# The last expert's rows kept on chip, and the residual summed by adding DMAs, in a one-core hybrid decoder step

## The reference

```python
def hier_moe(h, w_rg, b_rg, w_re, b_re, w_gate, w_up, w_down):
    ...
    g_sel = jnp.argmax(glog, axis=-1)                    # 1 of 4 groups
    ...
    top_v, top_i = lax.top_k(elog_sel, TOP_K_IN_GROUP)   # 2 of its 8 experts
    w_top = jax.nn.softmax(top_v, axis=-1) * p_g
    ...
    for e in range(N_EXPERTS):                           # 32, D_EXPERT = 512
        a = jax.nn.silu(hf @ w_gate[e]) * (hf @ w_up[e])
        y = y + gates[:, e:e + 1] * (a @ w_down[e]).astype(jnp.float32)
    ...

x = x + jnp.concatenate([yc, yp], axis=-1) @ w_out
x = x + hier_moe(rmsnorm(x, g_ffn), w_rg, b_rg, w_re, b_re, w_gate, w_up, w_down)
y = rmsnorm(x, g_final)
```

## Time and profile before

| what | value |
|---|---|
| median of 3 runs | 1410.45 us (1408.94 to 1411.17) |
| the profiled execution's own time | 1409.55 us |
| its span, first to last instruction | 1407.8 us |
| granted TensorE clock, mean | 0.978 of full speed |
| busy: TensorE / DVE / ACT / GpSimd | 1250.1 / 344.2 / 121.3 / 116.5 us |
| DMA | 464.61 MB, mean 330 GB/s |
| down product of the last expert ends | 1356.8 us |

### The profile page before, as it was taken

How to read it: one execution, slowest core, us unless ns; L and a number is a source line. 1 busy time by engine, 2 the same in 40 slices (tenths; PEclk the granted TensorE clock), 3 DMA queues, 4 the chain that set the end, 5 groups by cost and what they waited for, 6 DMA issues and landing times.

```text
span 1407.8 us, 16671 instructions
## 1 busy us (share of the span) xinstructions
PE 1250.1 (89%) x6515; PEld 711.9 (51%) x6515; DVE 344.2 (24%) x677; ACT 121.3 (9%) x242; POOL 116.5 (8%) x166
## 2 busy tenths in 40 slices
PE   8999989999999999989988898998898998898850
PEld 7777767777875444444333443433344343344210
DVE  4299953011251110110101011010111101011017
ACT  1100013000100000000000000000000000000003
POOL 2211143000000000000000000000000000000004
PEclk9999999999999999999999999999999999999985
DMA  8533423566349999999999999999999999999964
GB/s 233 163 120 119 153 86 107 198 247 243 133 190 373 421 423 426 423 422 421 424 423 423 424 421 423 422 423 424 422 423 422 424 421 424 420 423 419 379 193 124
DMA packets 100790, 464.61 MB, mean 330 GB/s; under 512 B 10095, under 2 KB 52207, under 8 KB 62115
## 3 DMA queue, kind: packets, MB, share of 16 engines
q1 hardware_dynamic: 95088, 455.89, 81.1%
q0 software_dynamic: 5392, 7.86, 1.8%
q10 hardware_dynamic: 283, 0.48, 0.1%
HBM read 456.67 MB, written 20.80 MB: 339 GB/s over the span
## 4 chain that ended last, share of the span: by engine, by line
DMA 50%; PE 35%; issue 7%; DVE 6%; SPq 1%; ACT 0%; ACTq 0%; DVEq 0%; POOLq 0%
DMA arena<-in_w_up_dram 48%; PE bank L546 13%; PE bank L699 13%; PE bank L718 3%; DVE arena L931 3%; PE bank L678 2%; PE bank L494 1%; DMA arena<-expert_rows 1%; SPq L381 1%; DMA pv<-in_pool_scale_dram 1%; PE bank L613 1%; DVE arena L1179 1%; DVE tn L891 0%; PE bank L583 0%; PE bank L630 0%
## 5 line engine op out<-in xcount | busy, mean ns | idle before, releaser
L699 PE MATMUL bank<-arena,stage 128*64 128x512 f32 x1920 | 429.4, 595 | 74.3 <-DMA arena<-in_w_up_dram 74.3
L699 PEld LDWEIGHTS bank<-arena,stage 128*64 128x64 f32 x1920 | 139.4, 137 | 356.7 <-issue 293.4
L546 PE MATMUL bank<-arena,stage 128*128 128x288 f32 x1280 | 315.0, 407 | 0.8 <-DVE arena L914 0.8
L546 PEld LDWEIGHTS bank<-arena,stage 128*128 128x128 f32 x1280 | 241.9, 190 | 66.3 <-issue 0.9
L678 PEld LDWEIGHTS bank<-x1w,x1r 96*128 96x128 f32 x1536 | 174.0, 192 | 26.0 <-issue 26.0
L678 PE MATMUL bank<-x1w,x1r 96*128 96x128 f32 x1536 | 180.2, 277 | 0.0
L1150 DVE TENSOR_TENSOR a_sb<-sl_sb,bank 128x256 f32<-128x256 f32 x32 | 19.4, 606 | 504.8 <-ACT sl_sb L843 504.8
L718 PE MATMUL bank<-arena,aT 128*64 128x512 f32 x512 | 113.4, 595 | 8.5 <-ACT aT L845 8.5
L1292 POOL DMA_INDIRECT expert_rows<-ysb,cur_d x32 | 31.3, 978 | 882.1 <-DVE ysb L1159 880.7
L931 DVE SCALAR_TENSOR_TENSOR arena<-arena,wdw 128x256 f32<-128x256 f32 x240 | 103.0, 501 | 0.0
L1159 DVE COPY ysb<-bank 128x512 f32<-128x512 f32 x32 | 22.1, 691 | 261.3 <-PE bank L718 261.3
(11 more groups left out here) (212 smaller groups left out, 494.2 us busy)
## 6 DMA issues: line engine op xcount, KB each, us to landing
arena<-in_w_gate_dram SPq DMA_DIRECT2D x112, 1024.0 KB, 17.0
arena<-in_w_up_dram SPq DMA_DIRECT2D x112, 1024.0 KB, 25.5
arena<-in_w_down_dram SPq DMA_DIRECT2D x30, 2048.0 KB, 21.5
xT<-in_w_down_dram SPq DMA_DIRECT2D x15, 2048.0 KB, 24.1
stage<-in_w_down_dram SPq DMA_DIRECT2D x15, 2048.0 KB, 25.5
stage<-in_w_in_dram SPq DMA_DIRECT2D x11, 2048.0 KB, 8.3
stage<-in_w_out_dram SPq DMA_DIRECT2D x8, 2048.0 KB, 8.1
stage<-in_w_gate_dram SPq DMA_DIRECT2D x16, 512.0 KB
```

The costliest lines, as they stand in the source:

```text
L546: last = pe.matmul(ps[bank][:, 0:NTOK], wsl[a][:, k, cc * P:(cc + 1) * P], rhs[:, k, :], start=(n == 0), stop=(n == KT - 1))
L699: last = pe.matmul(ps[4 + s][BLK * h:BLK * (h + 1), :], xgT[:, k, BLK * s:BLK * (s + 1)], w[:, :, 256 * h:256 * (h + 1)], start=(k == 0), ...
```

## The change

Four things are changed together.

1. **The residual goes to DRAM.** During the projection ACT copies each step's token rows from PSUM to a staging buffer and writes them to a new DRAM tensor `xres_dram` (12 copies of 96x512, four writes).
2. **Gate weights are applied at eviction.** The gate weights are worked out before the table; a second table `wslot` with the weight of each slot is multiplied by TensorE next to the first. ACT and DVE evict banks 2 and 3 with a multiplication by the slot's weight.
3. **The last expert's rows stay on chip**, in `ylast`. Its places in `yexp_dram` are filled with zeros by one more scatter, after the first pair. A one-hot matrix `lastT` (slots x tokens) is made in the last pair. After the experts TensorE multiplies it with `ylast`, 12 products of 96x512.
4. **DMAs add.** SP loads the residual rows into `yg` as each chunk comes free. GpSimd then issues six DMAs of 96 rows x 8 KB that add the rows of `yexp_dram` to them: the first expert row for the three tiles, then the second. DVE adds TensorE's products to the sum and applies norm and gain; GpSimd and ACT do no scaling of rows any more. The last tile goes out in two halves.

```diff
+PARTB = ((0, 1, 6, 7), (4, 5, 0, 1), (6, 7, 4, 5))
...
+        ylast = words(lns, 0, D // 2)
...
+            sp.wait_ge(xres_out, 16 * 4)
+            for t in range(TT):
+                sp.wait_ge(gu_used, 4 * (NE - 1) + t + 1)
+                sp.dma_start(yg[:, t, 0, :], xres_dram[t * TR:(t + 1) * TR, :]).then_inc(res_in[t], 16)
             sp.wait_ge(gu_used, 4 * NE)
             sp.dma_start(gfin, g_final[None, :].to_broadcast([TR, D])).then_inc(gfin_in, 16)
-
-            for s in range(2):
-                sp.wait_ge(y_out[s], 16 * PAIRS)
-            by_token = yexp_dram.rearrange("(t c) d -> t (c d)", c=4)
-            for t in range(TT):
-                for c in range(2):
-                    sp.dma_start(yg[:, t, c, :], by_token[t * TR:(t + 1) * TR, c * D:(c + 1) * D]).then_inc(yg_in[2 * t + c], 16)
-            for t in range(TT):
-                sp.wait_ge(scaled, t + 1)
-                if t == TT - 1:
-                    sp.wait_ge(out_ready, 1)
-                if t < TT - 1:
-                    sp.dma_start(y_prompt[0, t * TR:(t + 1) * TR, :], yg[:, t, 0, :]).then_inc(fin_out, 16)
-                else:
-                    sp.dma_start(y_prompt[0, t * TR:SEQ, :], yg[0:LASTP, t, 0, :]).then_inc(fin_out, 16)
-                    sp.dma_start(y_sample.rearrange("b t d -> (b t) d"), yg[LASTP:TR, t, 0, :]).then_inc(fin_out, 16)
-            sp.wait_ge(fin_out, 16 * (TT + 1))
+            for t in range(TT - 1):
+                sp.wait_ge(out_ready, t + 1)
+                sp.dma_start(y_prompt[0, t * TR:(t + 1) * TR, :], yg[:, t, 0, :]).then_inc(fin_out, 16)
+            t = TT - 1
+            ys_rows = y_sample.rearrange("b t d -> (b t) d")
+            for c in range(2):
+                sp.wait_ge(out_ready, TT + c)
+                d0, d1 = c * (D // 2), (c + 1) * (D // 2)
+                sp.dma_start(y_prompt[0, t * TR:SEQ, d0:d1], yg[0:LASTP, t, 0, d0:d1]).then_inc(fin_out, 16)
+                sp.dma_start(ys_rows[:, d0:d1], yg[LASTP:TR, t, 0, d0:d1]).then_inc(fin_out, 16)
+            sp.wait_ge(fin_out, 16 * (TT + 3))
...
+            pe.wait_ge(row_copy, 4 * TT)
...
-                        pe.wait_ge(dst_ready, 1)
+                        pe.wait_ge(dst_ready, 2)
...
+                    if last and s == 0:
+                        pe.wait_ge(last_ready, 1)
+                        for t in range(TT):
+                            ins = pe.transpose(ps[7][:, t * TR:(t + 1) * TR], last_hot[0][:, t, :], ident[0:TR, 0:TR])
+                        ins.then_inc(last_mm, 1)
...
-                            last = pe.matmul(ps[7][:, 0:NBLK], ohw[:, c, :], ohb[:, c, :], start=(c == 0), stop=(c == 2 * TT - 1))
-                        last.then_inc(tab_mm, 1)
+                            pe.matmul(ps[7][:, 0:NBLK], ohw[:, c, :], ohb[:, c, :], start=(c == 0), stop=(c == 2 * TT - 1))
+                        for c in range(2 * TT):
+                            mm = pe.matmul(ps[7][:, BLK:BLK + NBLK], ohw[:, c, :], ohg[:, c, :], start=(c == 0), stop=(c == 2 * TT - 1))
+                        mm.then_inc(tab_mm, 1)
...
+            pe.wait_ge(lastT_ready, 1)
+            pe.wait_ge(y0_ready, NE)
+            pe.wait_ge(y1_ready, NE)
+            for t in range(TT):
+                for m in range(2):
+                    if t:
+                        pe.wait_ge(part_added, 4 * t + 2 * m - 2 if t == 1 else 4 * t + 2 * m - 4)
+                    for h in range(2):
+                        pe.matmul(ps[PARTB[t][2 * m + h]][0:TR, :], lastT[BLK * h:BLK * (h + 1), t * TR:(t + 1) * TR],
+                                  ylast[BLK * h:BLK * (h + 1), 512 * m:512 * (m + 1)], start=True, stop=True).then_inc(part_mm, 1)
 
...
+            def row_squares(o):
+                for t in range(TT):
+                    if o or t:
+                        act.wait_ge(act_chain, TT * o + t)
+                    act.activation(ysbf[0:TR, 3 * 512:4 * 512], ps[2 + t][0:TR, :], ACT.Square,
+                                   accum_out=ssp3[:, t, o:o + 1]).then_inc(act_chain, 1)
+
+            def row_copies(o):
+                if o:
+                    act.wait_ge(xres_out, 16 * o)
+                for t in range(TT):
+                    if o == 3:
+                        act.wait_ge(row_evac, TT * o + t + 2)
+                    act.copy(ysbf[0:TR, 512 * t:512 * (t + 1)], ps[2 + t][0:TR, :]).then_inc(row_copy, 1)
+
+            def rows_out(o):
+                act.wait_ge(row_copy, TT * (o + 1))
+                act.dma_start(xres_dram.rearrange("(t r) d -> r t d", r=TR)[:, :, 512 * o:512 * (o + 1)],
+                              ysbf[0:TR, 0:512 * TT].rearrange("r (t d) -> r t d", t=TT)).then_inc(xres_out, 16)
+
+            for o in range(4):
                 act.wait_ge(row_mm, 4 * o + 4)
-                for t in range(TT):
-                    act.activation(ysb[0:TR, t % 2, (t // 2) * 512:(t // 2 + 1) * 512], ps[2 + t][0:TR, :], ACT.Square,
-                                   accum_out=dyn(ssp, 4 * t + o, 1, TR)).then_inc(act_chain, 1)
+                if o < 3:
+                    row_copies(o)
+                row_squares(o)
+                if o < 3:
+                    rows_out(o)
             act.wait_ge(act_in, 2)
             act.activation(sq[:, :], va[:, :], ACT.Sqrt).then_inc(sqrt_done, 1)
+            row_copies(3)
+            rows_out(3)
             act.wait_ge(act_in, 3)
             act.activation(r4b[:, :, :], r4[:, :, :], ACT.Exp).then_inc(exp_done, 1)
             act.wait_ge(act_in, 4)
             act.activation(ex[:, :, :], dl[:, :, :], ACT.Exp).then_inc(exp_done, 1)
 
 
-            def pair(i):
+            def pair(i, first=False, last=False):
                 for s in range(2):
                     n = 2 * i + s
-                    act.wait_ge(ysb_free[s], i + 1)
+                    if first and s == 0:
+                        act.wait_ge(xres_out, 16 * 4)
+                    if not (last and s == 1):
+                        act.wait_ge(ysb_free[s], i + 1)
                     act.wait_ge(gu_used, 4 * n + 4)
                     act.activation(sl_sb[:, :], ps[4 + s][:, 0:256], ACT.Silu).then_inc(sl_ready, 1)
                     act.wait_ge(at_mm, n + 1)
                     act.copy(aT[:, :], ps[6][:, 0:256]).then_inc(aT_ready, 1)
+                    if first and s == 0:
+                        act.wait_ge(dst_ready, 2)
+                    if last and s == 1:
+                        act.wait_ge(zero_out, 16)
                     act.wait_ge(wd_used, 4 * n + 4)
-                    act.copy(ysb[:, s, 0:512], ps[2][:, :]).then_inc(y0_ready, 1)
-
-            with act.Fori(0, PAIRS) as i:
+                    to = ylast[:, 0:512] if last and s == 1 else ysb[:, s, 0:512]
+                    act.activation(to, ps[2][:, :], ACT.Copy, scale=dyn(wslot, n, 1)).then_inc(y0_ready, 1)
...
+            act.activation(ssp[:, 0:1], ones[0:TR, 0:1], ACT.Sqrt)
+            for t in range(TT):
+                for c, to in ((0, ss), (1, ssb)):
+                    act.wait_ge(part_added, 4 * t + 4 if c else 4 * t + 3)
+                    act.activation(yg[:, t, 1, c * (D // 2):(c + 1) * (D // 2)], yg[:, t, 0, c * (D // 2):(c + 1) * (D // 2)],
+                                   ACT.Square, accum_out=to[:, t:t + 1]).then_inc(act_chain, 1)
...
+                dve.wait_ge(exp_done, 2)
+                link(dve.tensor_reduce(g2[:, :, :], r4b[:, :, :], AXX, ALU.add))
+                link(dve.reciprocal(pg[:, :, :], g2[:, :, :]))
+                link(dve.tensor_scalar(den[:, :, :], ex[:, :, :], 1.0, None, ALU.add))
+                link(dve.reciprocal(den[:, :, :], den[:, :, :]))
+                w0, w1 = wt[:, 0, :][:, :, None], wt[:, 1, :][:, :, None]
+                link(dve.tensor_tensor(w0, den[:, :, :], pg[:, :, :], ALU.mult))
+                ch.step(dve.tensor_tensor(w1, w0, ex[:, :, :], ALU.mult))
+
...
+                link(dve.tensor_tensor(ohg, ohb, wt[:, :, :].rearrange("p c t -> p (c t)")[:, :, None].to_broadcast([TR, C6, NBLK]), ALU.mult))
...
+                dve.tensor_copy(wslot[:, :], ps[7][:, BLK:BLK + NBLK]).then_inc(dst_ready, 1)
                 dve.tensor_scalar(dst_i[:, :], ps[7][:, 0:NBLK], half[:, :], float(PAD), ALU.add, ALU.add).then_inc(dst_ready, 1)
...
+            def add_part(t):
+                dve.wait_ge(rows_in[t], 32)
+                for m in range(2):
+                    for h in range(2):
+                        n = 4 * t + 2 * m + h
+                        seg = yg[:, t, 0, 1024 * h + 512 * m:1024 * h + 512 * (m + 1)]
+                        dve.wait_ge(part_mm, n + 1)
+                        dve.tensor_tensor(seg, seg, ps[PARTB[t][2 * m + h]][0:TR, :], ALU.add).then_inc(part_added, 1)
+
+            def norm(t):
+                dve.wait_ge(act_chain, 4 * TT + 2 * t + 2)
+                link(dve.tensor_tensor(va[:, t:t + 1], ss[:, t:t + 1], ssb[:, t:t + 1], ALU.add))
```

(60 more changed lines are left out.)

127 lines of the change are left out of this document (52 added, 75 removed).

## The result

| | before | after |
|---|---|---|
| median | 1408.91 us (20 runs) | 1411.03 us (20 runs, 1409.59 to 1414.43) |
| profiled execution, and its span | 1409.55, 1407.8 us | 1412.62, 1410.6 us |
| granted TensorE clock | 0.978 | 0.982 |

The ratio is 1.0017, with a 95% interval from 1.0011 to 1.0023: about 2 us, or 0.17%, slower. The forecast was 1409.2 us. The two profiled executions lie 2.8 us apart in span: that of the kernel after took 1.6 us more than its median, that of before 0.6 us more, so some 1 us of the 2.8 is of these two executions and not of the change.

The account below looks back on a forecast made before the run. DMA binds from 440 us until the experts end; before and in the tail, engine work counts. Span 1360.3 + 4 x 4.3 + 1.4 + 22.5 + 4.2 + 1.0 = 1406.6 us, time 1409.2; own range 1405 to 1413, overall 1399 to 1420.

Parts of the forecast that it names:

- ahead of the tail: Everything before the last expert's tail: row copies, squares, tables and zeros together add 1.0 us, range 0 to 3.3.
- four loads behind them: Three residual loads and g_final, queued on SP behind the last down weights: 1.86 us each, 7.4 us together.
- the start of the queue: Time from which the adding DMAs' work counts, after weights and four loads: 1360.3 us, bounds 1354 and 1363 us.
- nothing waits for these before 1373 us, so that costs 0: If late weights move TensorE's end to at most 1360 us, its first products come at 1362 us, at no cost.
- The price of adding: Cost of one 768 KB adding DMA in the tail: 4.3 us, between 2.96 and 5.9; 4.54 us gives no change.
- The two rivals that rested on it: An adding DMA takes 2.96 us, like a plain one (chance 0.31), or 5.9 us, like two (chance 0.25).
- 1/1.93: Skill's rule that an adding DMA runs at this fraction of a copy: 5.7 us per adding DMA, span 1413.6 us.
- The first wait of DVE: Sign in the tail: DVE's wait for the first tile's rows ends near 1379 us; before 1374 or after 1385 refutes.
- DVE's part: DVE's additions, norms and gains after the first tile's rows are in: 22.5 us, from 1378.9 to 1401.4 us.
- the extra table products: Six more TensorE products for the second table, 1.5 us, covered by the full DMA queue: 0, at worst 1.5 us.
- The 0.6 us for the squares that wait for each other: Ahead of routing, ACT's squares share a target and wait for one another, delaying norm and routing: +0.6 us.
- the early writes: Residual writes of 2.36 MB during projection: cost 0; rival that they hold up weights, up to 5.6 us, chance 0.04.

Follow-up runs that it names:

- the one that holds back: Kernel after, with SP issuing the three residual loads only once both halves of the last down weights have landed: 1409.49 us, ratio 1.0000.
- Under plain loads: Six adding DMAs made plain, overwriting loads: in the kernel after 1408.28 us; with the residual loads also held until the last down weights land 1408.47 us.
- the version on chip: Kernel after, with ACT copying the residual from x1r to yg, without row copies, their DRAM writes and the residual loads: 1398.60 us, ratio 0.9924.

## Why the prediction was wrong

The forecast was 1.8 us too low: the result is inside its range and inside the 0.2%, but on the other side of no change. That it was no more than 1.8 us is in part luck: it stood on a median of three runs, 1410.45 us, and 20 runs give 1408.91 us. The change itself was put at -1.2 us and measured at +2.1 us, 3.3 us off. Its sum, span 1406.6 us against 1410.6 us measured, goes term by term:

| term | forecast | measured | difference |
|---|---|---|---|
| ahead of the tail | +1.0 | +1.4 (weights issued 1328.5, before 1327.1) | +0.4 |
| last down weights, issue to landing | 25.8 | 32.6 | +6.8 |
| four loads behind them | 7.4 | 7.4 (1361.1 to 1368.5) | 0.0 |
| four adding DMAs | 17.2 | 16.8 (to 1385.3) | -0.4 |
| to the first landing, DVE from there | 1.4 + 22.5 | 1.4 + 20.0 | -2.5 |
| outputs | 4.2 | 3.9 | -0.3 |
| span | 1406.6 | 1410.6 | +4.0 |

In the column measured, some 1 us is of the profiled execution. The 1368.5 us are the landing of `g_final`, the last of the four loads (1350.05 + 19.9 = 1369.95 us), less the 1.4 us of the forecast from last packet to landing. The split between the second and the third row is bookkeeping: the loads were under way while the weights were, and the first adding DMA went out at 1363.3 us, beside them.

**The step that failed** is the start of the queue, put at 1360.3 us, "1363 us, if the loads slow the last weights by 3 us"; by the table it was 1368.5 us. Two of its terms were mis-sized.

First, the loads slowed the weights by 6.8 us, more than twice the bound. I had seen the late engines, and took them to be late only with their own weights. The mechanism was there as a bound; its size was taken from no row. Holding the loads back restored 25.3 us: shown.

Second, the four loads behind the weights were priced at the weights' pace, 1.86 us each. My own rows had the pace of this shape: 254 GB/s at a DMA share of 1.02, so 3.1 us each, 12.4 us instead of 7.4 us. In the kernel after, weights and loads together filled the engines at 225 to 227 GB/s. That this counts shows where the weights were on time: from the issue of the last weights to the first complete tile the forecast has 51.8 us, the kernel after 58.2 us, and the one that holds back 55.5 us. So holding gives back 2.7 of the 6.4 us, and 3.7 us stay although the weights land as forecast and an adding DMA costs 0.6 us less than forecast. How they divide between the price of the loads and the engines idle ahead of them, no run separates.

The other part, "nothing waits for these before 1373 us, so that costs 0", held in the time: TensorE did wait, 5.5 us, which I had excluded, and its product ended 9.7 us late, but DVE had to wait for the first rows until 1386.66 us anyway.

**The price of adding** was about right: 4.3 us forecast, 4.2 us from the rate in this kernel, 3.7 us with the loads held back, and nowhere near 2.96 or 5.9 us. The hit is in part luck: I had put it between two bounds and added half of a gap, and no run shows that half. The two rivals that rested on it, with 0.56 of the chance, are excluded. The rule of the Trainium skill, "Collectives: The Full Stack", section "The bandwidth ceiling: the fold count and why AG ≠ RS ≠ AR", is measured on the reduce step of a ring of four ranks against its copy step, and the page limits its model to rings. My prediction carried its 1/1.93 over to a load from DRAM with add; there it doesn't hold: against a plain load of this shape the ratio was 1.15 to 1.3.

The spacing forecast as the sign of it, "4.3 us", was seen as 4.6, 5.3, 4.0 and 3.7 us. **The first wait of DVE** ended at 1386.66 us, outside the 1374 to 1385 us that I had set as the test of the forecast. That DVE then works nearly without a break to the end was right.

**DVE's part** came out 2.5 us shorter. The additions took 2.48 us per tile (2.8 forecast), a norm 1.36 us (1.8), the gains 2.35 us each and the two halves together 2.5 us, as forecast. The products of the second tile, which I had hidden under DVE's steps, are on its path by 0.2 us: four products (x8 in the profile) at half clock start only when DVE's first additions have freed their banks (3.78 us in the chain). Under plain loads they cost 1.3 us. So that cover was thin.

**Ahead of the tail** the extra table products were put at 0, "at worst 1.5 us": they are handed on, 1.3 us of 2.1. The "full DMA queue" doesn't absorb a delay: an issue in it waits for TensorE to free a buffer, so one late issue makes the next ones late. The 0.6 us for the squares that wait for each other was 0.2 us: from the end of the projection's products, where the fillers start, to the routing's first product are 10.94 us in the kernel after and 10.73 us before (10.93 us in the version on chip, which has no row copies, so these aren't the cause). The evictions with a scale cost nothing (DVE's took 751 instead of 691 ns, with the lag of TensorE 2.1 us at 441 us and 2.3 us at 1336 us), and so did the early writes.

## What to carry to other kernels

That two thirds of the DMA engines look idle doesn't make a load free that is put behind a late stream in the same queue: here it slowed the stream's last pieces by 6.8 us, and landed only after them. Price it by its shape's own rate (here 96 rows of 8 KB at 246 GB/s, not 422), and keep on chip what is on chip already: 2.36 MB of residual sent out and back cost 12.4 us, more than the 10.3 us that the rest of the change brought. No run put the residual loads in another queue, so whether that would have spared the weights isn't known. And a full DMA queue hands a delay on, if its issues wait for the engine that was late.

## What the runs showed of the hardware that I had not expected

- An adding DMA of 768 KB into 96 partitions cost 3.7 to 4.2 us of all engines against 3.2 us for a plain one, far less than twice the plain one. Its issue on GpSimd took 0.79 us against 0.51 us.
- Behind a stream of weights with late engines, a load of 768 KB landed 20.2 to 22.9 us after its issue; issued after that stream, the first of three took 5.6 us. It made the stream's last 2 MB land 32.6 us after issue instead of 25.3.
- TensorE's granted clock, 2.4 GHz for nearly all of 300 to 1340 us, fell to 1.2 GHz (0.5) for a few us at 395, 441 or 564 us, in eight of the twelve traces of this study and at one or two of the places in each, although these programs are nearly the same there.
